# Two transformer blocks on one core: the second block's first units from the unscaled residual, and its feed and load order rewritten

## The reference

```python
def first_block(x, ...):                       # twice, then a last norm
        h = rms_norm(x, ln1_gain[l])
        proj = h @ w_in[l]                     # three kinds of mixer on its parts
        x = x + mixed @ w_out[l]
        h = rms_norm(x, ln2_gain[l])
        x = x + jnp.square(jax.nn.relu(h @ w_up[l])) @ w_down[l]
    return rms_norm(x, final_gain)

def hybrid_layer(x, c_act, ...):               # second block, twice
    sh1, sc1, g1, sh2, sc2, g2 = jnp.split(c_act @ w_ada + b_ada, 6, axis=-1)
    h = rmsnorm(x, norm1_w) * (1 + sc1) + sh1
    u = h @ w_in                               # pool, conv, q, k, v, gate logits
    x = x + g1 * (merged @ w_out)
    h2 = rmsnorm(x, norm2_w) * (1 + sc2) + sh2
    x = x + g2 * ((silu(h2 @ w_gate) * (h2 @ w_up)) @ w_down)
```

## Time and profile before

| what | us |
|---|---|
| median of 3 runs (1469.65 to 1471.19) | 1469.85 |
| the profiled execution | 1471.11 |
| its span, first to last instruction | 1469.3 |
| PE busy | 1450.8 (99%) |
| PE weight loads busy | 1371.4 (93%) |
| DVE busy | 1118.5 (76%) |
| ACT busy | 805.2 (55%) |
| POOL busy | 70.0 (5%) |
| DMA, mean | 202 GB/s |

### The profile page before, as it was taken

How to read it: one execution, slowest core, us unless ns; L and a number is a source line. 1 busy time by engine, 2 the same in 40 slices (tenths; PEclk the granted TensorE clock), 3 DMA queues, 4 the chain that set the end, 5 groups by cost and what they waited for, 6 DMA issues and landing times.

```text
span 1469.3 us, 27367 instructions
## 1 busy us (share of the span) xinstructions
PE 1450.8 (99%) x11112; PEld 1371.4 (93%) x11112; DVE 1118.5 (76%) x2023; ACT 805.2 (55%) x1428; POOL 70.0 (5%) x76
## 2 busy tenths in 40 slices
PE   9999999999999999999999999999999999999999
PEld 9998999889989999888999998999889999999987
DVE  7888787886888787887886688778878657876654
ACT  6585777444575677434555455444454554654442
POOL 0000000000000000000030220000003003000000
PEclk9999999999999999999999999999999999999999
DMA  9332487884233477883545454767844445455551
GB/s 332 152 138 84 174 296 280 328 309 163 108 140 126 158 285 275 323 306 144 183 162 198 179 188 155 257 251 267 341 173 144 172 144 179 166 174 198 174 198 60
DMA packets 43132, 296.96 MB, mean 202 GB/s; under 512 B 5248, under 2 KB 6016, under 8 KB 7552
## 3 DMA queue, kind: packets, MB, share of 16 engines
q1 hardware_dynamic: 42592, 295.20, 55.4%
q10 hardware_dynamic: 416, 0.02, 0.0%
HBM read 293.62 MB, written 1.05 MB: 201 GB/s over the span
## 4 chain that ended last, share of the span: by engine, by line
PE 86%; DVE 9%; ACT 3%; issue 1%; DMA 1%; SPq 0%; DVEq 0%; ACTq 0%
PE acc L843 19%; PE acc L844 19%; PE acc L845 19%; PE acc L849 13%; PE acc L850 7%; DVE wL L1855 3%; ACT wH L1467 1%; PE ps_t L1011 1%; PE ps_s L998 1%; PE ps_s L996 1%; PE acc L1101 1%; DMA ring<-stream 1%; PE acc L1336 0%; PE acc L1331 0%; DVE x L2557 0%
## 5 line engine op out<-in xcount | busy, mean ns | idle before, releaser
L1855 DVE TENSOR_TENSOR wL<-ring,wH 128x1024 fp32r<-128x1024 f32 x444 | 550.1, 1246 | 215.5 <-ACT wH L1467 207.9
L843 PE MATMUL acc<-hH,wH 128*128 128x256 f32 x2048 | 592.2, 289 | 6.3 <-DVE wL L1855 5.2
L844 PE MATMUL acc<-hL,wH 128*128 128x256 f32 x2048 | 579.3, 283 | 0.0
L845 PE MATMUL acc<-hH,wL 128*128 128x256 f32 x2048 | 579.1, 283 | 0.0
L1467 ACT ACTIVATE wH<-ring 128x1024 fp32r<-128x1024 f32 x444 | 464.1, 1051 | 189.3 <-PE acc L850 117.2
L843 PEld LDWEIGHTS acc<-hH,wH 128*128 128x128 f32 x2048 | 392.4, 192 | 13.5 <-DVE wL L1855 8.0
L844 PEld LDWEIGHTS acc<-hL,wH 128*128 128x128 f32 x2048 | 392.7, 192 | 3.3 <-issue 2.6
L845 PEld LDWEIGHTS acc<-hH,wL 128*128 128x128 f32 x2048 | 392.5, 192 | 0.0
L849 PE MATMUL acc<-aHL,wH 128*128 128x512 f32 x512 | 179.6, 398 | 0.0
L850 PE MATMUL acc<-aHL,wL 128*128 128x256 f32 x512 | 141.1, 281 | 0.0
L849 PE MATMUL acc<-a2HL,wH 128*128 128x512 f32 x352 | 123.1, 397 | 0.0
(11 more groups left out here) (370 smaller groups left out, 2053.8 us busy)
## 6 DMA issues: line engine op xcount, KB each, us to landing
ring<-stream SPq DMA_DIRECT2D x276, 1024.0 KB, 4.8
cst<-consts SPq DMA_DIRECT2D x1, 1363.0 KB, 15.6
x<-xin SPq DMA_DIRECT2D x4, 256.0 KB, 5.0
out<-x SPq DMA_DIRECT2D x4, 256.0 KB, 4.2
onc<-once SPq DMA_DIRECT2D x1, 516.0 KB, 16.0
v1all<-vec SPq DMA_DIRECT2D x1, 355.0 KB, 9.7
v2all<-vec SPq DMA_DIRECT2D x1, 330.0 KB, 18.3
nv<-pos SPq DMA_DIRECT2D x1, 256.0 KB, 5.0
```

The costliest lines, as they stand in the source:

```text
L843: pe.matmul(out, w[0], y[0], start=first, stop=False)
L844: pe.matmul(out, w[0], y[1], start=False, stop=False)
L845: return pe.matmul(out, w[1], y[0], start=False, stop=last)
L1855: TTN(wL[:, n % SPLIT, :], ring[:, g % RING, half * UNIT:(half + 1) * UNIT], wH[:, n % SPLIT, :].bitcast(F32), ALU.subtract).then_inc(lo_r ...
```

## The change

- The first four units of the second block (`RAW`) run from unscaled `x` times the gain, with the shift as columns beside it (258 columns). ACT and DVE make these parts during the down product before (`part_raw`, `rest_raw`). The sum of squares stands inside the second unit (`project_around`). The results are scaled by `scale_raw` and squared by `raw_squares`. The `kept_busy` calls there are gone; the normalised `h` is needed from the fifth unit on, and is first put into a buffer of its own (`zs`).
- The final norm of the first block goes over `x` inside the attention loop of the first layer, one chunk a head.
- Before the feed-forward part six units run unscaled in place of four, the sum of squares stands inside the second, and the feeds are spread over `norm_out` at chunks 4 and 6.
- Three gate units run ahead of the attention loop, and 15 stay in it.
- In each layer of the first block 21 `ada` tiles ride in place of 16 (9 in the up part, 12 in the down part; before 7 and 9), in the second block 6 in place of 16. The modulation is formed at the first down block, not the fifth or the seventh.
- The last block of each down product uses three 256-column matmuls a step, so that one `evac` operation fewer follows it. The last stores are split finer.
- At the start the first tile is loaded in two halves, the positions after it; 34 matmuls on ones in place of 40, and none in place of seven before the second layer of the first block. The matrix `rotr`, which nothing used, is gone.

Cut to its core:

```diff
-AHEAD = 4
+AHEAD = 6
+RAW = 4
...
+ADA_FIRST = [("up", j) for j in (3, 4, 6, 7, 9, 10, 12, 13, 15)] + [("down", j) for j in (0, 1, 3, 4, 5, 7, 8, 9, 11, 12, 13, 14)]
 ADA_AFTER = {
-    (1, 0): [("up", j) for j in (3, 5, 7, 9, 11, 13, 15)] + [("down", j) for j in (0, 2, 3, 5, 6, 8, 9, 11, 12)],
-    (1, 1): [("up", j) for j in (3, 5, 7, 9, 11, 13, 15)] + [("down", j) for j in (0, 2, 3, 5, 6, 8, 9, 11, 12)],
-    (2, 0): [("gate", 4), ("gate", 9)] + [("gu", j) for j in (4, 7, 10, 13, 16, 19, 21)]
-    + [("down", j) for j in (0, 2, 3, 5, 6, 8, 9)],
+    (1, 0): ADA_FIRST,
+    (1, 1): ADA_FIRST,
+    (2, 0): [("gate", 4), ("gate", 9)] + [("gu", j) for j in (12, 15, 18, 21)],
...
+LEAD = 3
 def gates_at(i):
-    steps = NH2 + 2
-    return range(-(-len(HEAD_ORDER) * i // steps), -(-len(HEAD_ORDER) * (i + 1) // steps))
+    steps, n = NH2 + 2, len(HEAD_ORDER) - LEAD
+    return range(LEAD - (-n * i // steps), LEAD - (-n * (i + 1) // steps))
...
-SQUARES_AT = {3: 0, 5: 1, 7: 2, 9: 3}
-REFINE_AT = {4: 0, 6: 1, 8: 2, 10: 3}
-ROTATE_AT = {6: 0, 8: 1, 10: 2, 12: 3}
+SQUARES_AT = {4: 0, 6: 1, 8: 2, 10: 3}
+REFINE_AT = {5: 0, 7: 1, 9: 2, 11: 3}
+ROTATE_AT = {7: 0, 9: 1, 11: 2, 13: 3}
...
+        def raw_gain(L, n):
+            return fgains[:, 1, n:n + 1] if L == 0 else modsall[:, L, n:n + 1]
...
+                    sp.dma_start(ring[:, 0, 0:UNIT], stream[row_of(0)][:, 0:UNIT]).then_inc(first_in, 16)
+            def load(g):
+                if g == 0:
+                    sp.dma_start(ring[:, 0, UNIT:TILE], stream[row_of(0)][:, UNIT:TILE]).then_inc(got[0], 16)
...
+            parts = [(0, 2), (2, 4), (4, 6), (6, 7), (7, 8)]
+            for first, end in parts:
...
+                        if n < KC - 1:
+                            last = wide_product(a, w, both[:, k, :], k == 0, k == kf - 1)
+                        else:
+                            last = split_product(a[:, 0:S], w, (both[:, k, 0:S], both[:, k, S:2 * S]), k == 0, k == kf - 1)
...
+            def project_around(names, width, y, ready, then):
+                parts = [blocks(next_unit()) for _ in names]
+                banks = [open_acc(name) for name in names]
+                def chunks(i, cs):
+                    (wh, wl), a = parts[i], banks[i]
+                    for c in cs:
+                        if i == 0:
+                            ready(c)
+                        last = split_product(a[:, 0:width], (wh[:, c, :], wl[:, c, :]), y(c), c == 0, c == KC - 1)
+                        if c == KC - 1:
+                            last.then_inc(acc_full, 1)
+                chunks(0, range(KC - 1))
+                chunks(1, range(SIDE))
+                chunks(0, range(KC - 1, KC))
+                then()
+                chunks(1, range(SIDE, KC))
...
+                project_around(names[:2], PLAIN, lambda c: (zh[:, c, :], zl[:, c, :]),
+                               lambda c: pe.wait_ge(plain_low, L * (KC + 1) + (c + 2)),
+                               lambda: sum_squares("ss2", norm2(L, 1)))
...
+            def project_raw(i, name, L):
+                wh, wl = blocks(next_unit())
+                a = open_acc(name)
+                for c in range(KC):
+                    last = split_product(a[:, 0:PLAIN], (wh[:, c, :], wl[:, c, :]), (hH[:, c, :], hL[:, c, :]),
+                                         c == 0, c == KC - 1)
+                    if i == RAW - 1 and c < KC - 1:
+                        last.then_inc(raw_read, 1)
+                last.then_inc(acc_full, 1)
...
-                    kept_busy(40)
+                    kept_busy(34)
...
-                    kept_busy(7)
...
-                kept_busy(2)
-                sum_squares("ss1", norm2(L, 0))
-                kept_busy(10 if L == 0 else 14)
-                project_side_by_side(STEPS2[:SIDE], normed(H2), hs)
                 for i, u in enumerate(STEPS2):
                     if u in ("v0", "v1"):
                         for t in range(TT):
                             project_tokens("v", int(u[1]), t, 256)
-                    elif i >= SIDE:
-                        project(u, hs)
+                    elif i == 0:
+                        project_around(STEPS2[:2], PLAIN, lambda c: (hH[:, c, :], hL[:, c, :]),
+                                       lambda c: pe.wait_ge(raw_low, L * (KC + 1) + (c + 2)),
+                                       lambda: sum_squares("ss1", norm2(L, 0)))
+                    elif i < RAW:
+                        if i >= 2:
+                            project_raw(i, u, L)
+                    else:
+                        project(u, hs, ready=normed(H2) if i == RAW else None)
...
+                for n in HEAD_ORDER[:LEAD]:
+                    project(f"g{n}", hs)
...
+            def part_raw(n, L):
+                if n == 0:
+                    shift = modall[:, L, 0:KC].unsqueeze(2).to_broadcast([P, KC, PLAIN - S])
+                    act.activation(hH[:, :, S:PLAIN], shift, ACT.Copy).then_inc(raw_high, 1)
+                act.activation(hH[:, n, 0:S], x[:, n, :], ACT.Identity, scale=raw_gain(L, n)).then_inc(raw_high, 1)
...
+                def take_raw(i):
+                    a = full(A2, STEPS2[i], L)
+                    act.activation(raw[:, i, :], a[:, 0:S], ACT.Copy)
+                    act.activation(raw_shift[:, i:i + 1], a[:, S:S + 1], ACT.Copy)\
+                        .then_inc(acc_drained[A2.bank(STEPS2[i])], 1)
+                def raw_squares(b):
+                    act.wait_ge(raw_scaled, L * (RAW // 2) + (b + 1))
+                    for k in (2 * b, 2 * b + 1):
+                        last = act.activation(sq2[:, k, :], raw[:, k, :], ACT.Square, bias=raw_shift[:, k:k + 1])
+                    last.then_inc(raw2_sq, 1)
+                    for k in (2 * b, 2 * b + 1):
+                        act.activation(raw[:, k, :], raw[:, k, :], ACT.Identity, bias=raw_shift[:, k:k + 1])
+                def released(c):
+                    if c < KC - 1:
+                        act.wait_ge(raw_read, L * (KC - 1) + (c + 1))
+                    else:
+                        act.wait_ge(acc_full, A2.full(STEPS2[RAW - 1], L))
+                take_raw(0)
                 root(A2, "ss1", L)
+                feed(1 + SPLIT)
                 if L == 0:
                     act.wait_ge(plain_full, 1)
                     act.activation(ny[:, 1, :], ps_o[:, 0:S], ROOT, scale=1.0 / D).then_inc(plain_y, 1)
-                feed(SPLIT)
-                round_h(L * (2 * KC) + H2, lambda c: modall[:, L, c:c + 1])
+                for i in range(1, RAW - 1):
+                    take_raw(i)
+                    feed(min(i + 1, 2) + SPLIT)
+                round_h(L * (2 * KC) + H2, lambda c: modall[:, L, c:c + 1], lambda c: zs[:, c, :], {}, released)
+                raw_squares(0)
+                feed(3 + SPLIT)
+                take_raw(RAW - 1)
+                feed(4 + SPLIT)
...
+                def opened(n):
                     act.wait_ge(plain_out, AHEAD * L + (2 * n + 1))
-                    link(act.activation(r4[n], plain_at[2 * n], ACT.Tanh, scale=0.5, bias=shifted_by[:, 4 + n:5 + n]))
-                    act.activation(r4[n], r4[n], ACT.Identity, scale=0.5, bias=shifted_by[:, 6:7]).then_inc(tanh_ready, 1)
-                    feed(60 + AHEAD - 1 + SPLIT)
-                for n in range(AHEAD // 2):
+                    link(act.activation(r4[n], plain_at[2 * n], ACT.Tanh, scale=0.5, bias=by_half_shift(2 * n)))
+                    act.activation(r4[n], r4[n], ACT.Identity, scale=0.5, bias=a_half).then_inc(tanh_ready, 1)
...
+                feed(60 + 4 + SPLIT)
+                opened(0)
+                feed(60 + 5 + SPLIT)
+                opened(1)
+                pair_high(0)
+                opened(2)
+                feed(60 + 6 + SPLIT)
+                pair_high(1)
+                pair_high(2)
...
+            def rest_raw(n, L):
+                if n == 0:
+                    shift = modall[:, L, 0:KC].unsqueeze(2).to_broadcast([P, KC, PLAIN - S])
+                    dve.wait_ge(raw_high, L * (KC + 1) + 1)
+                    TTN(hL[:, :, S:PLAIN], shift, hH[:, :, S:PLAIN].bitcast(F32), ALU.subtract).then_inc(raw_low, 1)
+                dve.wait_ge(raw_high, L * (KC + 1) + (n + 2))
+                STT(hL[:, n, 0:S], x[:, n, :], raw_gain(L, n), hH[:, n, 0:S].bitcast(F32), ALU.mult, ALU.subtract)\
...
+                for c in range(KC):
+                    STT(zs[:, c, :], x[:, c, :], raw_gain(L, c), rstd, ALU.mult, ALU.mult).then_inc(h_pre, 1)
+                feed(1 + SPLIT)
+                scale_raw(0)
+                feed(2 + SPLIT)
+                for c in range(KC):
+                    dve.wait_ge(hh_ready, L * (2 * KC) + H2 + (c + 1))
+                    STT(hL[:, c, 0:S], zs[:, c, :], mod[:, c:c + 1], hH[:, c, 0:S].bitcast(F32), ALU.add, ALU.subtract)\
+                        .then_inc(h_ready, 1)
+                feed(3 + SPLIT)
+                scale_raw(1)
...
```

(16 more changed lines are left out.)

243 lines of the change are left out of this document (129 added, 114 removed).

## The result

| | before | changed |
|---|---|---|
| median of the runs, us | 1470.52 (1469.65 to 1471.28, 4 runs) | 1448.02 (1447.39 to 1451.15, 4 runs) |
| ratio to before, 95% interval | | 0.9851 (0.9834 to 0.9868) |
| profiled execution, us | 1471.1 | 1447.4 |
| its span, us | 1469.3 | 1445.6 |

The changed kernel is faster by 22.5 us.

The account below looks back on a forecast made before the run. PE, busy 99% of the span, was taken as the bound, with gains only where its starts lag the matmul pace. Terms summed to -16.6 us: 1454.5 for a profiled execution, 1453.3 for the median, range 1449.5 to 1459.5.

Parts of the forecast that it names:

- narrow last down blocks: Last down blocks: 108 steps of three narrow matmuls cost between 0 and +1.1 us, taken as +0.5.
- first hand-over and first heads: Into block 2's first layer: 6.9 us removable, 0.4 of new wait, so -6.4; the first heads a separate small gain.
- second hand-over and heads: Into block 2's second layer: 6.9 us between matmuls, 0.67 stays, 1.1 of new wait, so -5.1; heads separate.
- feed-forward parts: Before each feed-forward part: three waits for wL become one of 1.4 us at the eleventh unit; -2.4 in all.
- rival B: Without dummies, remaining short waits may bring the lower clock, four places at half clock: 1459 us; chance 0.05.
- rival A: DVE cannot keep up behind the hand-overs, and nothing is gained before the feed-forward parts: about 1459.5 us; chance 0.15.
- rival D: Everything fits: no wait at hand-overs or before feed-forward parts, start gains 2 us: 1447.5 to 1450; chance 0.10.
- Three gate units ahead of the loop take the table load and `y1L` off that path, -0.6: First attention head: PE's 0.27 us wait for the weights in each layer goes, -0.6 for both layers.
- The units ahead absorb 8.6: Block 1's down parts: units ahead of PE cover 8.6 us of lateness from the added ada tile loads.
- rival C: Block 1's down parts: the ring runs dry as ada loads make weights late, 26 us for both layers, 1479; chance 0.04.
- in block 1 ACT's waits stay with PE and not with the DMA: Sign that the forecast is right: in block 1, ACT waits for PE, not for loads.
- All the rest is matmuls at full pace, which the change keeps.: Everywhere outside the listed places: matmuls keep their pace, 0.12 us for 256 columns, so no term for them.

Follow-up runs that it names:

- The kernel with the distance of before: Changed kernel with h, mt, mg, y and the down product's rows placed a multiple of 256 bytes from the split weights: 1456.26 us, ratio 0.9904.
- the kernel with wider rows: Kernel before without rotr and with rows of 258 columns in hH and hL, 256 used, order of before: 1463.81 us, ratio 0.9954.

## Why the forecast was wrong, step by step

The kernel with the distance of before has the changed order and the old pace, so its stages can be set against the forecast's terms one by one; 'now' is the changed kernel where the pace does not blur it. The column at the old pace compares one profiled execution of each kernel.

| term | forecast | at the old pace | now |
|---|---|---|---|
| start | -0.5 | -0.7 | first sum 0.96 earlier |
| dummies, block 1 layer 1 | -1.4 | -1.7 | -1.5 by putting them back |
| narrow last down blocks | +0.5 | +1.3 | +1.0 |
| wait before the last down block (ring) | 0 | +1.8 | +0.3 (0.3 to 0.9 in five kernels) |
| first hand-over and first heads | -6.7 | -5.6 | hand-over -6.4 |
| second hand-over and heads | -5.4 | -5.7 | hand-over -5.1 |
| feed-forward parts | -2.4 | -2.9 | two waits, 1.6 a layer |
| tail | -0.7 | -0.8 | -0.8 |
| sum | -16.6 | -14.3 | |
| pace of all the rest | 0 | 0 | -8.2 |

**Right.** The hand-overs are as walked: 0.26 of new wait where I had 0.4, and 1.07 where I had 1.1. No clock fell in the profiled execution (mean granted clock 1.000), so rival B did not come there. One of the four runs, the one of 1451.15 us, has a mean granted clock of 0.999; a short fall may lie behind its 3 us, and no trace of it is kept. DVE kept up at the hand-overs, so rival A did not come. The measured time lies in the band of rival D, 1447.5 to 1450, but that is luck: D asked for no wait at the hand-overs, none before the feed-forward parts and 2 us at the start, and the changed kernel has waits of 0.26, 1.07 and 1.2 us and a start 0.96 earlier. The eleventh unit waits (1.23, forecast 1.4), though a small wait of 0.38 at another unit was not foreseen.

**Mis-sized.** Four steps. 'Three gate units ahead of the loop take the table load and `y1L` off that path, -0.6': the second head of the first layer waited 1.01 us instead. I had put the slots at nothing because PE waited in none of them; the list of DVE, with two `ada` multiplications and a step of the final norm in one slot, was in the order and would have told it. 'The units ahead absorb 8.6' for the `ada` tiles in the down parts: rival C's mechanism is there, at 0.3 to 1.8 us in one layer in place of 26 in both, because ACT waits for the ring (19.3 us in all in that layer, where it waited for PE alone before) and the cover is almost used up. The sign 'in block 1 ACT's waits stay with PE and not with the DMA' did not hold. 'A step may cost up to 0.01 more, I take +0.5' for the narrow blocks: 1.0 us measured, near the upper bound. And the feed-forward parts gave a little more, -2.9 for -2.4. Together they made the reordering 2.3 us weaker than forecast: with the old pace the kernel takes 1456.3 us, 3.0 above the forecast and inside its range. (Two small sums in the forecast are off by 0.1 to 0.2 us, without effect: the way of the last residual adds up to 2.1 and not 2.2, rival A to 1459.7 and not 1459.5.)

**Failed.** 'All the rest is matmuls at full pace, which the change keeps.' This step put the pace of all the rest at a change of 0, and it measured -8.2 us. 0.1200 us was not the full pace, only the pace at this distance between two tensors. I took it for a constant of the matmul because every row of before showed it: all of before's tensors happened to stand at distance 0, but for the `plain` rows. Two things could have warned me. The `plain` matmuls have 258 columns and took 0.1200 us as well, and two columns more at no cost suggest that something else than the columns sets the pace of the 256. And the page of the Trainium skill that I cited (TensorE: Matmul & The Clock Gate, section Back-to-back issue gap) gives 0.109 for 256 columns. I left out that the same section calls this the gap of an isolated matmul, which counts too little at small sizes where every matmul has its own weight load. So 0.109 was not to be expected here, but the 11 ns above it, in each of some 8000 matmuls, were a figure to explain; I wrote 'the trace agrees only roughly' and passed on. The runs here come down to 0.1133, never to 0.109.

Not tried: the hand-overs with fewer raw units, and the feed-forward part with the taking of four units; the code did not allow either by a number alone. Their terms rest on the traces.

## What to carry to other kernels

A change to the size of any tensor moves all tensors behind it, and that can be worth as much as the order of the work: list what the diff does to addresses, and where one pitch holds in the whole trace, ask what it depends on before calling it full pace. For float32r products on this chip, measure the pitch against the distance, modulo 256 bytes, between the moving rows and the weights; an empty tensor of 192 bytes was enough here. And when a piece of work is moved out of a busy slot, look at the list of the engine in the slot that gets it: here the gate units ahead of the loop removed one wait and made another, and so did the `ada` tiles moved to the feed-forward part. A difference of 1 us in one profiled execution is no proof of a gain as long as a wait elsewhere varies by as much.

## What the runs showed of the hardware

- The pitch of a float32r matmul of 256 columns with its own weight load is between 0.1133 and 0.1233 us by the distance between the moving rows and the weights in SBUF; it is the same, 0.1200, at 0, 256, 512 and 1024 bytes. At 0 and at 128 bytes it stayed 0.1198 and 0.1186 with DVE and ACT busy on other addresses. With 258 columns it was 0.1196 to 0.1202 at every distance tried. The Trainium skill (SBUF — State Buffer, section A bandwidth-pool intuition that's wrong) gives TensorE a second, independent port for weight loads; if moving rows and weights were read independently in every respect, their distance would not matter, and here it does. By what mechanism was not tested.
- At the same distance of 192 bytes whole stretches run at 0.1178 and others at 0.1133, within one execution, even for the same code in two layers. It changes only where the row of matmuls is interrupted by 0.20 us or more from start to start (163 changes in three traces). What sets the pace that follows is open.
- Wide steps (one matmul of 512 columns and one of 256) depend on it less: 0.353 us at distances 0 and 192, 0.351 in the changed kernel, and between 0.347 (16 and 32 bytes) and 0.353 by themselves.
- Behind the same wait of 1.60 us the granted clock was 0.50 for 3 us in the profiled execution of the kernel before and 1.00 in that of the kernel with wider rows, which was 1.1 us shorter there.
